# A three-layer float32 model on one core: the RMS scale per token moved from the projections' operand to their read-out

## The reference, cut to what matters

```python
def rmsnorm(x, g):
    y = x * lax.rsqrt(jnp.mean(x * x, axis=-1, keepdims=True) + EPS)
    return y * g

def conv_ffn(h, w_up, conv_w, conv_b, w_down):
    a, b = jnp.split(h @ w_up, 2, axis=-1)
    a = causal_conv3(a, conv_w) + conv_b
    return (jax.nn.silu(a) * b) @ w_down
...
x = x + gla_layer_mix(rmsnorm(x, g_mix[0]), ...)
x = x + conv_ffn(rmsnorm(x, g_ffn[0]), ...)
shared = rmsnorm(x, g_kv) @ w_kv        # and its compressed blocks
x = x + nsa_layer_mix(rmsnorm(x, g_mix[1]), shared, ...)
x = x + conv_ffn(rmsnorm(x, g_ffn[1]), ...)
x = rmsnorm(x, g_final)
proj = rmsnorm(x, w_norm_mix) @ w_mix_in    # short conv, delta rule, stick-breaking attention
x = x + concat(y_sc, y_gdn, y_sb) @ w_mix_out
u = causal_dwconv(rmsnorm(x, w_norm_ffn) @ w_ffn_up, w_ffn_conv)   # both halves
gate, val = split(u)
x = x + (silu(gate) * val) @ w_ffn_down
return rmsnorm(x, w_norm_final)
```

## Time and profile before

| | |
|---|---|
| median of 3 runs | 2188.32 us (2187.66 to 2189.27) |
| the profiled execution | 2189.8 us |
| its span | 2188.1 us |
| mean granted clock of PE | 0.971 |
| PE, PEld busy | 94%, 75% of the span |
| DVE, ACT, POOL busy | 47%, 38%, 6% |
| HBM traffic | 76 GB/s over the span |

### The profile page before, as it was taken

One profiled execution on the slowest core, in us unless ns is written; L12 is line 12 of the kernel. 1 busy time (PEld: TensorE's weight loads), 2 busy tenths in 40 slices (PEclk: granted clock), 3 DMA queues, 4 the chain that ended last, 5 costly groups with the idle time before them and its releaser, 6 DMA issues. The chain is left out here.

```text
span 2188.1 us, 27456 instructions
## 1 busy us (share of the span) xinstructions
PE 2062.3 (94%) x10545; PEld 1640.5 (75%) x10545; DVE 1037.0 (47%) x1555; ACT 839.7 (38%) x1301; POOL 132.4 (6%) x136
## 2 busy tenths in 40 slices
PE   6999779999999999888999999999998899999998
PEld 5686647888878787556788878778786678888786
DVE  7421742644453452653544543344655347565532
ACT  4533153423232454543432333343654244333323
POOL 0000001000000100440000000100041010000001
PEclk9999799999999999899999999999999899999999
DMA  4420012333322251002233323232110033323221
GB/s 159 136 77 1 1 39 83 110 97 97 100 91 96 64 151 60 1 1 77 87 97 96 96 87 106 68 90 85 58 40 2 1 95 98 105 86 107 87 96 39
DMA packets 135400, 167.69 MB, mean 77 GB/s; under 512 B 28306, under 2 KB 102535, under 8 KB 135303
## 3 DMA queue, kind: packets, MB, share of 16 engines
q1 hardware_dynamic: 134598, 166.12, 24.0%
q10 hardware_dynamic: 705, 0.25, 0.0%
HBM read 164.24 MB, written 2.10 MB: 76 GB/s over the span
## 5 line engine op out<-in xcount | busy, mean ns | idle before, releaser
L178 PE MATMUL bank<-h_hi,w_hi 128*128 128x512 f32 (+1 forms) x2256 | 873.9, 387 | 19.6 <-DVE h_lo L315 6.6
L179 PE MATMUL bank<-h_lo,w_hi 128*128 128x512 f32 (+1 forms) x2256 | 872.5, 387 | 0.0
L180 PE MATMUL bank<-h_hi,w_lo 128*128 128x512 f32 (+1 forms) x2256 | 872.2, 387 | 0.0
L142 DVE TENSOR_TENSOR w_lo<-raw,w_hi 128x1024 fp32r<-128x1024 f32 x306 | 371.7, 1224 | 778.8 <-ACT w_hi L136 777.5
L136 ACT CAST w_hi<-raw 128x1024 fp32r<-128x1024 f32 x306 | 319.8, 1052 | 758.1 <-PE bank L178 748.3
L178 PEld LDWEIGHTS bank<-h_hi,w_hi 128*128 128x128 f32 x2256 | 424.5, 188 | 114.0 <-issue 15.7
L180 PEld LDWEIGHTS bank<-h_hi,w_lo 128*128 128x128 f32 x2256 | 424.6, 188 | 85.9
L179 PEld LDWEIGHTS bank<-h_lo,w_hi 128*128 128x128 f32 x2256 | 424.5, 188 | 85.0
L259 POOL TENSOR_TENSOR keep<-keep 128x512 f32<-128x512 f32 x30 | 41.9, 1396 | 1498.3 <-ACT keep L252 1496.6
L165 PE MATMUL bank<-level,ident 128*128 128x512 f32 x174 | 84.3, 633 | 10.7 <-ACT h_words L2577 3.8
L1198 ACT COPY keep<-bank 128x512 f32<-128x512 f32 x88 | 51.9, 589 | 75.5 <-PE bank L180 74.4
(11 more groups left out here) (441 smaller groups left out, 1778.9 us busy)
## 6 DMA issues: line engine op xcount, KB each, us to landing
raw<-in_w_up SPq DMA_DIRECT2D x176, 256.0 KB, 2.9
raw<-in_w_down SPq DMA_DIRECT2D x44, 512.0 KB, 3.1
raw<-in_w_ffn_up SPq DMA_DIRECT2D x88, 256.0 KB, 3.0
raw<-in_w_mix_in SPq DMA_DIRECT2D x24, 512.0 KB, 3.7
raw<-in_w_ffn_down SPq DMA_DIRECT2D x22, 512.0 KB, 3.4
raw<-in_w_mem_kv SPq DMA_DIRECT2D x16, 512.0 KB, 5.9
raw<-in_a_w_in SPq DMA_DIRECT2D x16, 512.0 KB, 3.7
raw<-in_a_w_out SPq DMA_DIRECT2D x8, 512.0 KB, 6.5
```

Of the source, the lines that this page charges most:

```text
L142: dve.tensor_tensor(k.w_lo[n % RING][:, :], k.raw[n % RING][:, :], k.w_hi[n % RING][:, :].bitcast(F32), ALU.subtract)\
L178: a = pe.matmul(out, sh, mh, start=first, stop=False)
L179: pe.matmul(out, sh, ml, start=False, stop=False)
L180: c = pe.matmul(out, sl, mh, start=False, stop=last)
```

## The change

The norm is linear in rstd, so that h @ w = rstd * ((x * gain) @ w) for each token. The change uses this in the five stages that begin with such a norm.

- The operand is now x * gain, split at once (`act_next`, `dve_next`); no rstd is needed for it. `dve_sums`, `act_next`, `dve_next` and `pool_sums` work tile by tile, and a `Handoff` carries the counts over the stage change: after an out projection tiles 0 to 3 are split and 0 to 5 summed and squared in the old stage, after an FFN likewise; tiles 6 and 7 are summed, and 4 to 7 split, in the new one. The warm-up matmuls and the norm ahead of the first product are gone from these stages.
- The sum over features is one ones matmul (`pe_sums`), put between two chunks of the new stage's first group; rstd follows while PE goes on.
- The read-outs of transposed tiles multiply by rstd on DVE, where ACT copied before; for the other side of the one-sided FFNs that is an added operation (`other_side`), and the gate product reads it from SBUF. Where a tile has tokens in partitions (the value tiles), ACT scales by a column, which four one-column matmuls make from rstd (`pe_rstd_columns`).
- The double norm is closed: the gains are multiplied at set-up (`k.mixed`), and the second mean square is a weighted sum of the same squares (`weighted`), so that both norms' scales come from one pass; the final-normed x itself is made later, for the residual.
- In the mix stage ACT's list changes with it: silus, read-out 24 and table users stand in another order.

The diff, cut to its core:

```diff
def before(i, kk):
+        if kk == 0 and rstd_by is not None and t + i in (6, 7):
+            pe.wait_ge(k.rstd_ready.sem, k.rstd_ready.at(rstd_by))
...
+        if aside is not None and c == aside[0]:
+            aside[1]()
...
+def dve_sums(k, dve, ho, tiles):
+    for kk in tiles:
+        dve.wait_ge(k.tile_full.sem, ho.full + kk + 1)
+        dve.tensor_tensor(k.xT[:, kk, :], k.xT[:, kk, :], bank(k, kk)[:, :], ALU.add).then_inc(k.tile_free.sem, 1)
+def act_next(k, act, ho, gain, tiles, squares, free=None):
+    for kk in sorted(set(tiles) | set(squares)):
+        act.wait_ge(k.tile_free.sem, ho.added + kk + 1)
+        if kk in tiles:
+            if free is not None:
+                act.wait_ge(k.ring.used, free(kk))
+            act.activation(k.h_hi[:, kk, :], k.xT[:, kk, :], ACT.Copy, scale=gain(kk)).then_inc(k.h_rounded.sem, 1)
+        if kk in squares:
+            act.activation(k.sq[:, kk, :], k.xT[:, kk, :], ACT.Square, scale=1024 ** -0.5).then_inc(k.sq_ready.sem, 1)
+def dve_next(k, dve, ho, gain, tiles):
+    for kk in tiles:
+        dve.wait_ge(k.h_rounded.sem, ho.rounded + kk + 1)
+        dve.scalar_tensor_tensor(k.h_lo[:, kk, :], k.xT[:, kk, :], gain(kk), k.h_hi[:, kk, :].bitcast(F32),
+                                 ALU.mult, ALU.subtract).then_inc(k.h_ready.sem, 1)
+def pool_sums(k, pool, ho, tiles, last):
+    for kk in tiles:
+        pool.wait_ge(k.sq_ready.sem, ho.squared + kk + 1)
+        before = k.sq[:, 0, :] if kk == 1 else k.sums[:, :]
+        ins = pool.tensor_tensor(k.sums[:, :], before, k.sq[:, kk, :], ALU.add)
+        if kk == last:
+            ins.then_inc(k.sq_added.sem, 1)
+        else:
+            k.pool_chain.link(pool, ins)
+def pe_sums(k, pe, ho, b=7):
+    pe.wait_ge(k.sq_added.sem, ho.summed + 1)
+    pe.matmul(bank(k, b)[:, :], k.ones[:, :], k.sums[:, :], start=True, stop=True).then_inc(k.sums_full.sem, 1)
...
+def pe_rstd_columns(k, pe, b=7):
+    for tt in range(4):
+        mm = pe.matmul(bank(k, b)[:, tt:tt + 1], k.rstd[:, tt * P:(tt + 1) * P], k.ident[:, 0:1], start=True, stop=True)
+    mm.then_inc(k.sums_full.sem, 1)
...
+            g_last, g_mix = (k.vecs[:, VEC_ROWS[n]:VEC_ROWS[n] + 8] for n in ("g_final", "w_norm_mix_2"))
+            dve.wait_ge(out, len(jobs) + VEC_TILES)
+            dve.tensor_tensor(k.mixed[:, 0:8], g_last, g_mix, ALU.mult)
+            L(dve.tensor_tensor(k.mixed[:, 8:16], g_last, g_last, ALU.mult))
+            L(dve.tensor_scalar(k.mixed[:, 8:16], k.mixed[:, 8:16], 1e-6, None, ALU.add))
...
-            act_load_ln(k, act)
-            act_new_squares(k, act, range(4))
-            split_hi(k, act, first + 10)
-            act_new_squares(k, act, range(4, 8))
+            for c in range(2):
+                pair = (2 * c, 2 * c + 1)
+                act_next(k, act, ho, gain, pair, pair, lambda kk: first + 5 + kk // 2)
+                split_hi(k, act, first + 9 + c)
+            act_next(k, act, ho, gain, (), (4, 5))
...
-            pe_new_sums(k, pe)
-            pe_used(k, pe)
...
+            split_lo(k, dve, first + 7)
+            dve_sums(k, dve, ho, range(4))
+            split_lo(k, dve, first + 8)
+            for c in range(2):
+                dve_next(k, dve, ho, gain, (2 * c, 2 * c + 1))
+                split_lo(k, dve, first + 9 + c)
+            dve_sums(k, dve, ho, (4, 5))
...
+                    if g == 1 and i == 2 and kk == 0:
+                        pe.wait_ge(k.rstd_ready.sem, k.rstd_ready.at(1))
...
+                    if g == 0 and c == 2:
+                        pe_sums(k, pe, now)
...
-            pe_warm(k, pe, 5)
...
-            act_norm(k, act)
+            act_next(k, act, now, gain, range(4, 8), (6, 7))
             split_hi(k, act, first + 4)
-            act.wait_ge(cleared.sem, cleared.at(2 * sides))
...
+                act_next(k, act, ho, after, range(4), range(6), lambda kk: down0 + 20)
...
-            dve_norm(k, dve, gain)
+            dve_sums(k, dve, now, (6, 7))
+            dve_next(k, dve, now, gain, range(4, 8))
             split_lo(k, dve, first + 4)
+            dve.wait_ge(cleared.sem, cleared.at(2 * sides))
+            dve.wait_ge(k.rstd_ready.sem, k.rstd_ready.at(1))
...
-                    dve.wait_ge(padded.sem, plus(padded.at(sides * f + s + 1), reg, 4 * sides))
                     dst, src = acc[s][f % 2], pad[s][f % 2]
+                    dve.wait_ge(k.tile_full.sem, plus(k.tile_full.at(2 * f + s + 1), reg, 8))
+                    k.dve_chain.link(dve, dve.tensor_tensor(src[:, 2:514], bank_of(f, s)[:, :], k.rstd[:, :], ALU.mult))
...
+            def other_side(f, reg):
+                dve.wait_ge(k.tile_full.sem, plus(k.tile_full.at(2 * f + 2), reg, 8))
+                dve.tensor_tensor(acc[1][f % 2], bank_of(f, 1)[:, :], k.rstd[:, :], ALU.mult).then_inc(conv_b.sem, 1)
...
+                for o in range(6):
+                    dve_sums(k, dve, ho, (o,))
+                    if 1 <= o < 5:
+                        dve_next(k, dve, ho, after, (o - 1,))
...
+            for t in range(4):
+                src, dst = full(t), kv2[t // 2][:, t % 2, :]
+                dve.tensor_tensor(dst[0:64, 0:512], src[0:64, :], k.rstd[0:64, :], ALU.mult).then_inc(kv_shift, 1)
+                freed(dve.tensor_tensor(dst[64:P, 0:511], src[64:P, 1:512], k.rstd[64:P, 1:512], ALU.mult))
...
             for half in range(2):
-                dve_split(k, dve, lambda kk: h2[:, kk, :], 8 + 4 * half, tiles=range(4 * half, 4 * half + 4))
+                for kk in range(4 * half, 4 * half + 4):
+                    dve.wait_ge(k.h_rounded.sem, k.h_rounded.at(8 + kk + 1))
+                    dve.scalar_tensor_tensor(k.h_lo[:, kk, :], k.xT[:, kk, :], g_mix(kk), k.h_hi[:, kk, :].bitcast(F32),
+                                             ALU.mult, ALU.subtract).then_inc(k.h_ready.sem, 1)
...
-            pe_warm(k, pe, 5)
-            t = pe_group(k, pe, 0, [feature_tile(k, m * P) for m in range(4)], 0)
+            t = pe_group(k, pe, 0, [feature_tile(k, m * P) for m in range(4)], 0, (2, lambda: pe_sums(k, pe, now)))
+            pe.wait_ge(k.rstd_ready.sem, k.rstd_ready.at(1))
+            pe_rstd_columns(k, pe)
...
-            dve_normed(k, dve, x, x, VEC_ROWS["g_final"], 512)
-            dve.wait_ge(k.rstd_ready.sem, k.rstd_ready.at(2))
-            dve_normed(k, dve, lambda kk: k.sq[:, kk, :], x, VEC_ROWS["w_norm_mix_2"], 512, 0)
+            dve_sums(k, dve, now, (6, 7))
+            dve_next(k, dve, now, gain, range(4, 8))
+            split_lo(k, dve, first + 4)
+            for kk in range(8):
+                dve.wait_ge(k.sq_ready.sem, now.squared + kk + 1)
+                share = k.mixed[:, 8 + kk:9 + kk]
+                if kk == 0:
+                    L(dve.tensor_scalar(weighted, k.sq[:, kk, :], share, None, ALU.mult))
+                    continue
+                ins = dve.scalar_tensor_tensor(weighted, k.sq[:, kk, :], share, weighted, ALU.mult, ALU.add)
+                if kk < 7:
+                    L(ins)
+            ins.then_inc(k.sq_added.sem, 1)
             dve.wait_ge(ab_split, 1)
             dve.tensor_tensor(ab_lo[:, :, 0:8], w_ab[:, :, :], ab_hi[:, :, 0:8].bitcast(F32), ALU.subtract).then_inc(ab_split, 1)
...
+            for t in range(4):
+                freed(dve.tensor_tensor((k.scb if t < 2 else k.scc)[:, t % 2, :], full(t), k.rstd[:, :], ALU.mult))
+            dve.wait_ge(k.rstd_ready.sem, k.rstd_ready.at(2))
+            for kk in range(8):
+                dve.scalar_tensor_tensor(x(kk), x(kk), k.vec(VEC_ROWS["g_final"] + kk), k.sums[:, :], ALU.mult, ALU.mult)
+            split_lo(k, dve, first + 11)
...
+                freed(dve.tensor_tensor(src[:, 3:515], full(11 + n + n // 4 - n // 8), k.rstd[:, :], ALU.mult))
...
+            dve.wait_ge(k.tile_free.sem, k.tile_free.at(25))
+            for t in range(25, 29):
+                freed(dve.tensor_tensor(k.zT[:, t - 25, :], full(t), k.rstd[:, :], ALU.mult))
...
+            act.wait_ge(k.sums_full.sem, k.sums_full.at(1))
+            L(act.activation(k.rstd[:, :], bank(k, 7)[:, :], ACT.Ln, bias=k.eps2[:, 0:1]))
+            L(act.activation(k.sums[:, :], bank(k, 6)[:, :], ACT.Ln, bias=k.eps[:, 0:1]))
+            for r in (k.rstd, k.sums):
+                act.activation(r[:, :], r[:, :], ACT.Exp, scale=-0.5).then_inc(k.rstd_ready.sem, 1)
...
-            read_out(20, 5)
+            for n in range(8, 11):
+                silu(n)
+            read_out(24, 1)
+            silu(11)
...
-            read_out(25, 4)
+            for t in range(25, 29):
+                act.wait_ge(k.tile_free.sem, k.tile_free.at(t + 1))
+                act.activation(k.zT[:, t - 25, :], k.zT[:, t - 25, :], ACT.Silu)
...
-            pe_warm(k, pe, 4)
-            pe_norm_sums(k, pe)
-            pe_warm(k, pe, 5)
+            def both_sums():
+                pe.wait_ge(k.sq_added.sem, now.summed + 2)
+                pe.matmul(bank(k, 6)[:, :], k.ones[:, :], k.sums[:, :], start=True, stop=True)
```

(7 more changed lines are left out.)

304 lines of the change are left out of this document (164 added, 140 removed).

## The result

The changed kernel took 2201.3 us (median of five runs, 2200.8 to 2202.2) against 2188.3: a ratio of 1.0058, 95% interval 1.0047 to 1.0069. The forecast was 2154.7, so both the number and the sign were wrong. Yet everything that the forecast said of the stage changes happened.

What follows compares the result with a forecast made beforehand. TensorE, busy 94% of the span, was taken as the bound; 44.5 us gained at five stage changes, less losses, left 33.6 us, so 2188.3 us would become 2154.7 us, range 2145 to 2167.

Steps and rivals of the forecast that it cites:

- 21.8 us at the pace above: Third FFN, steady state: a group of 96 matmuls takes PE 21.8 us, hiding DVE's 17.3 us of work.
- five rivals: Forecast itself 60%, waits feeding each other 17%, read-outs queueing less 13%, a stage change staying open 6%, slower 3%.
- rival 5: Slower: DVE becomes the bound in the third FFN, needing 24.9 us a group to eat the gain; 3%.
- the other new waits: Half clock behind new waits other than the mix stage's 3.0 us one: 0.5 us lost together.
- The five stage changes: Where the next stage begins with a norm: closing them saves 7.94, 8.32, 7.94, 19.60 and 8.22 us, 52.0 in all.
- Rival 4: A stage change stays open because an engine arrives late; at 4 us in each of five, 2174 us; 6%.
- The third FFN's turn from up to down: Two more products ahead of the first lo and later gates make PE wait longer: 1.6 us lost.
- The one-sided turns: One-sided FFNs, up to down: 0.1 us lost each, 0.2 us in all; PE's wait stays 1.54 us.
- The NSA stages: Input stage: lo's queueing behind activation splits cost 1.0 us, besides 0.95 for the ones matmul and 0.9 for one-column matmuls.
- the terms (1.9 + 0.9 + 1.7 + 0.5): Mix stage, beginning: ones matmuls 1.9, one-column matmuls 0.9, waits for lo's and banks 1.7, POOL contention 0.5 us.
- 4.2 for the waits: Mix stage, end: late z read-outs make PE wait amid and behind eight ones matmuls; decay matmuls start 4.2 us later.
- POOL beside DVE: Mix stage: some seven DVE instructions meeting POOL's adds take 0.5 us more each, 3.5 together; 0.5 us lost.

Runs made afterwards that it cites:

- experiment 6: Changed kernel with its two new small tiles put behind the weights, so every other tile lies where the kernel before has it: 2154.2 us, ratio 0.9831.
- 8: Changed kernel with padding behind mixed_gains, so the weights lie 256 bytes further from h than in the kernel before: 2152.0 us, ratio 0.9825.
- experiments 10 to 13: Changed kernel with one tile moved against h_hi: w_lo by 32 bytes 2194.4 us, w_hi by 32 2185.7, h_lo by 32 2189.8, h_lo by 256 2154.2.

## Why the prediction was wrong, and what of it was right

**The step that failed** is one that the prediction never wrote as a term: that all matmuls which the change leaves alone keep their pace, "21.8 us at the pace above" for a group of 96. They did not; the pace went from 0.2266 to 0.2339 us, 47 us in all, because two small tiles that take 32 and 64 bytes slipped between h and the weights. Over the whole trace, wherever the clock was full, it was 0.2342 in the delivered kernel and 0.2269 in experiment 6; times 6768 that is 50 us. Of this the delivered kernel got some 7 us back, because less of its time was at half clock (a mean granted clock of 0.970 over 2199.6 us against 0.966 over 2155.6, that is 66 against 73 us lost). That leaves 43 of the 44.0 us between the two spans. None of the five rivals has it; rival 5 (DVE bound in the third FFN) had the right sign for another reason, and there is no trace of it.

The whole diff has the two new `sb(...)` allocations, and the kernel before shows that tiles are laid one behind the other in the order of these calls. The profile of before could not have told that 96 bytes cost anything, since all its matmuls run at one distance; but it could have been seen that the addresses of the operands of 6768 matmuls change. That was worth a rival with a bound. The Trainium skill would have been no help for its size: SBUF — State Buffer, Operand start alignment, says that an operand must start at a multiple of its element size and that its measurements timed nothing; Who interferes with whom, on the same page, says that TensorE has a read port for the moving operand and an independent one for the weight load, and waits for no one. The runs here show PE's pace depending on the places of the two operands, at full granted clock and with no wait in the trace. In this case the measurement decides.

**The number of experiment 6** (2154.2 beside a forecast of 2154.7) is closer than the terms were. The stretches in the table below miss by up to 1.8 us, in both directions, and parts of the mix stage by about 2; and the execution in the trace, the slowest of four (2157.4), gained 32.5 us by its span where the medians give 35.3.

**The terms of the sum, one by one.** Experiment 6 is the kernel that the prediction was about, and can be compared with before stretch by stretch. The starts of the stages, PE's timeline, experiment 6 (and the earlier trace rows with the rows below for before):

```profile
332.63 0.47 PE L178 MATMUL bank<-h_hi,w_hi 128*128 128x512 f32 x1 [2.32 <-PEq L744]
...
376.87 0.47 PE L178 MATMUL bank<-h_hi,w_hi 128*128 128x512 f32 x1 [0.47 <-PEq L846]
...
739.43 0.47 PE L178 MATMUL bank<-h_hi,w_hi 128*128 128x512 f32 x1 [0.48 <-PEq L1182]
...
995.11 0.47 PE L178 MATMUL bank<-h_hi,w_hi 128*128 128x512 f32 x1 [2.97 <-PEq L1731]
...
1039.35 0.47 PE L178 MATMUL bank<-h_hi,w_hi 128*128 128x512 f32 x1 [0.47 <-PEq L846]
...
1401.90 0.47 PE L178 MATMUL bank<-h_hi,w_hi 128*128 128x512 f32 x1 [0.47 <-PEq L1182]
...
1725.59 0.47 PE L178 MATMUL bank<-h_hi,w_hi 128*128 128x512 f32 x1 [3.38 <-DVE h_lo L399]
...
1769.87 0.47 PE L178 MATMUL bank<-h_hi,w_hi 128*128 128x512 f32 x1 [0.47 <-PEq L846]
...
2138.89 4.53 PE L165 MATMUL bank<-level,ident 128*128 128x512 f32 x10 [0.44 <-PEq L1182]
```

and those of before that were not shown yet:

```profile
332.69 0.47 PE L178 MATMUL bank<-h_hi,w_hi 128*128 128x512 f32 x1 [2.32 <-PEq L654]
...
1005.80 0.47 PE L178 MATMUL bank<-h_hi,w_hi 128*128 128x512 f32 x1 [2.98 <-PEq L1603]
...
1057.96 0.47 PE L178 MATMUL bank<-h_hi,w_hi 128*128 128x512 f32 x1 [0.39 <-DVE h_lo L315]
...
1753.10 0.47 PE L178 MATMUL bank<-h_hi,w_hi 128*128 128x512 f32 x1 [3.38 <-DVE h_lo L315]
...
2172.18 4.53 PE L165 MATMUL bank<-level,ident 128*128 128x512 f32 x10 [0.44 <-PEq L1090]
```

Each line of the table is the difference of two such starts, in us; gains are positive.

| stretch, from one first product to the next | before | exp. 6 | gain | forecast, from the prediction's terms |
|---|---|---|---|---|
| start to first out-projection | 332.69 | 332.63 | 0.1 | -0.6 (set-up) |
| out-projection and its stage change | 52.19 | 44.24 | 7.95 | 7.94 |
| first FFN and its stage change | 369.89 | 362.56 | 7.3 | 8.32 - 0.95 - 0.1 = 7.3 |
| NSA input and attention | 251.03 | 255.68 | -4.65 | -0.95 - 0.9 - 1.0 = -2.85 |
| second out-projection | 52.16 | 44.24 | 7.9 | 7.94 |
| second FFN and its stage change | 381.18 | 362.55 | 18.6 | 19.60 - 0.95 - 0.1 = 18.55 |
| mix and delta stages | 313.96 | 323.69 | -9.7 | -1.9 - 0.9 - 1.7 - 4.2 + 0.4 - 1.0 - 0.5 = -9.8 |
| third out-projection | 52.44 | 44.28 | 8.2 | 8.22 |
| third FFN | 366.64 | 369.02 | -2.4 | -0.95 - 1.6 = -2.55 |
| final norm to the end of the span | 15.9 | 16.7 | -0.8 | 0 |
| clock behind the other new waits | | | | -0.5 |
| sum | 2188.1 | 2155.6 | 32.5 | 33.6 |

- **The five stage changes**, the largest term of the forecast, came out within 0.1 us each, as far as the stretches part them from the other terms: all engines arrive before PE, and the restart is 0.47 or 0.48 (forecast 0.44). Rival 4 is gone. The ones matmul in the stream costs about what was reckoned (L2300 to L2301 in the mix stage 0.86 us).
- **The third FFN's turn from up to down.** PE's wait is 3.23 us at 2013.64 where it was 1.92; its loss, with the ones matmul, is 2.4 against 2.55. In the kernel as delivered there is a second wait behind it, for the gate:

```profile
2054.51 0.50 PE L178 MATMUL bank<-h_hi,w_hi 128*128 128x512 f32 x1 [3.06 <-DVE h_lo L1394]
...
2061.72 0.50 PE L178 MATMUL bank<-h_hi,w_hi 128*128 128x512 f32 x1 [1.32 <-DVE keep L1367]
```

The prediction had PE arrive there just as late as the gate, because it ran at half clock in between; in the delivered kernel it did not fall to half clock after its 3.06 us (granted clock 1.00 over 2054.5 to 2057.5) and came early.
- **The one-sided turns** stayed at 1.54, as forecast.
- **The NSA stages were mis-sized** by 1.8 us. The input stage lost 2.4 (forecast 2.85): its wait grew from 1.46 to 1.71 only. The attention stage behind it, whose code is the same, lost 2.3 more, at a lower granted clock. Windows of all engines, before and then experiment 6, each from the same matmul on (columns: PE, PEld, DVE, ACT, POOL busy, granted clock, DMA):

```profile
816.09:860.00 43.91, 43.91 (x196) 36.08 (x197) 10.59 (x9) 16.81 (x30) 0.00 (x0) 0.96 0.32 97
...
900.00:950.00 50.00, 42.95 (x320) 28.66 (x320) 30.52 (x103) 26.81 (x88) 21.99 (x20) 0.90 0.01 1
```

```profile
803.12:847.20 44.08, 44.02 (x190) 35.80 (x191) 15.57 (x17) 11.38 (x21) 0.00 (x0) 0.93 0.31 97
...
888.00:938.40 50.40, 43.62 (x316) 29.32 (x318) 30.75 (x105) 26.93 (x89) 21.98 (x20) 0.87 0.01 1
```

0.03 of 44 us is 1.3 us, and 0.03 of 50 is 1.5; between these two stretches the clock was higher than before (0.92 over 20.3 us against 0.83 over 20.0), which gives 1.8 us back, so that over the whole stage the clock accounts for about 1.3 of the 2.3 us. Where the rest went is open. The 0.5 us for "the other new waits" was too small for what these stages and the delta stage lost at half clock.
- **The mix stage's total is right partly by luck.** Its beginning lost 3.1 us (138.82 to the ones matmuls of the end before, 141.95 now), not the 5.0 of the terms (1.9 + 0.9 + 1.7 + 0.5): DVE's waited read-out cost PE 0.50 us at one bank and no wait at the first lo. Its end:

```profile
1543.85 3.59 PE L2326 MATMUL bank<-scratch,ones 128*128 128x512 f32 x8
1549.94 5.34 PE L2326 MATMUL bank<-scratch,ones 128*128 128x512 f32 x8 [2.49 <-DVE keep L2173]
1555.12 2.06 PE L2331 MATMUL bank<-triu,keep 128*128 128x128 f32 x17
```

From the first ones matmul to the decay matmuls 11.27 us, where it was 6.87: 4.4 against a forecast of 4.8 (4.2 for the waits, 1.0 for the half clock that follows, 0.4 given back by the gate product), with the wait in the middle of the eight matmuls as said (2.5, not 3) and half clock behind it; the second wait, of 1 us behind the eight, did not come. Behind it the delta stage, untouched, lost 2.2 us that I had not reckoned, again at a lower clock in one part of it: 0.91 over 58.6 us where before had 0.94 over 58.0.
- **POOL beside DVE** was misread from the row. The 2.38 us for two products are one of 0.68 us, begun 0.1 us before one of POOL's adds ended, and one of 1.78, begun in the middle of the next add: not 0.5 us each, but 1.1 for the second alone. It was the same here. DVE's and POOL's rows at the beginning of the mix stage, experiment 6:

```profile
1402.95 5.87 DVE L292 SCALAR_TENSOR_TENSOR h_lo<-xT,mixed_gains,h_hi 128x512 fp32r<-128x512 f32 x4
```

```profile
1403.52 6.45 POOL L301 TENSOR_TENSOR tail<-tail,keep 128x512 f32<-128x512 f32 x4
```

One by one, the first lo, which began 0.57 us before POOL's first add, took 0.74 us, and the three that began during an add 1.79, 1.78 and 1.79: 1.04 more each. POOL's first add took 1.33 and the others 1.63, 1.63 and 1.62. Their ends alternate: each of the three lo's ends about 0.55 us after an add did, and the next add about 1.15 us after the lo. The Trainium skill (SBUF — State Buffer, Who interferes with whom) has the later of two such instructions stand still for all of the earlier; by that a lo that meets an add would take up to the 1.40 us of an add more, an estimate. The 1.04 is nearer to this rule than to the 0.5 of the forecast, and the alternating ends fit it. But only three lo's and a split of weights (2.31 us, not 1.23) met an add, 4.2 us in all, where the forecast had seven instructions and 3.5 us; and it cost nothing, since the sums stood just in time: DVE's last step ended at 1418.11, and PE made them without a wait at 1418.34, 16.4 us into the stage, forecast 16.3.
- **The clock.** Half clock followed the wait of 2.49 us in the mix stage (0.50 over 1549.9 to 1552.9) and partly the one of 3.23 in the third FFN (0.58 over 2013.6 to 2016.6).

## What is shown and what stays open

Shown: 96 bytes of padding cost the kernel before 50.8 us; moving h with the weights takes that away; putting the tiles back gives the change its forecast gain; distances that are multiples of 256 bytes (0, 256 and 512 more than before, and h_lo by 256) have the pace 0.2267; every other one tried (32, 64, 96 and 128 beyond such a multiple) has 0.2317 to 0.2339; one tile of the four out of step is enough; and what the other engines do meanwhile makes no difference. The version that beats both kernels is experiment 6, or 8 (2154.2 and 2152.0 us, which is the same within their intervals).

Shown too: the time follows the pace once this is averaged over the whole trace and not over the five stretches. Sorted by it, the changed kernels have 0.2269 (2152.0 to 2154.9 us), 0.2319 (w_hi by 32; 2185.7), 0.2326 (h_lo by 32; 2189.8), 0.2326 and 0.2328 (128; 2190.3 and 2190.1), 0.2332 (64; 2193.9), 0.2332 (w_lo by 32; 2194.4) and 0.2342 (96; 2201.3). In the kernel before, 0.2268 goes to 0.2333 (32) and 0.2342 (96) for 43 and 51 us.

Open: why. That the read of the streamed operand and the load of the next stationary one get in each other's way at some distances fits the order of the three steps in experiments 10 to 13, but no run shows it by itself; it does not explain why the loss spreads over all three steps, nor why one tile off costs nearly as much as two. Distances of 160 to 224 bytes were not tried.

## What to carry to other kernels

When a change adds even one small tile, compare where all the large operands lie before and after, and keep the distances between those that TensorE streams and loads. Padding costs no time, only bytes of SBUF, and here it was worth more than the whole rewrite. When the result contradicts the forecast, first measure the pace of work that the change leaves alone: if that has moved, no argument about the changed code can explain the result. And before a good change is thrown away, run it with the old layout.

## What the hardware showed that I had not expected

- fp32r matmuls of 128x128 by 512 columns, with no waits and a granted clock of 1.00, follow each other in 0.2267 us if h_hi, h_lo, w_hi and w_lo lie whole multiples of 256 bytes apart, and in 0.2317 to 0.2339 us if one of them does not: 2.2 to 3.2%. In the busy share (94% in both kernels) nothing of this shows; it shows in the number of records in a stretch of fixed length.
- One wait can be followed by half clock or not: 3.06 us in the delivered kernel was not, 3.23 us in experiment 6 at the same place partly was.
- In two kernels whose attention stage has the same instructions, half clock came at other places in it and cost about 1.3 us more in one; the wait ahead of it in the input stage was 1.46 us in the one and 1.71 in the other. What moved the places is not shown.
- Beside GpSimd's adds, VectorE instructions with two inputs in SBUF took 1.79 us instead of 0.75, and the two engines' instructions ended in turn. The mean over a row of several hides this, when some of them met no add.
